# Moving squares ahead of the last piece, a key block across a phase border, and splitting a maximum

## The reference, cut to what matters

```python
def layer(x, cond, l, rope, ctx_kv):
    sh_a, sc_a, g_a, sh_f, sc_f, g_f = adaln_params(cond, mod_w[l], mod_b[l])
    o, k, v = token_mixer(modulate(x, norm_attn[l], sh_a, sc_a), l, rope, ctx_kv)
    x = x + g_a * o
    f = conv_ffn(modulate(x, norm_ffn[l], sh_f, sc_f), w_up[l], conv_w[l], conv_b[l], w_down[l])
    return x + g_f * f, k, v

def modulate(x, norm_w, shift, scale):
    return rms_norm(x, norm_w) * (1.0 + scale) + shift       # rms_norm: mean of squares over the 1024 channels

def conv_ffn(h, w_up, conv_w, conv_b, w_down):
    u = conv(h @ w_up); g, val = jnp.split(u, 2, axis=-1)
    return (jax.nn.silu(g) * val) @ w_down

# grouped-query attention, per head: q, k normed and rotated
p = jax.nn.softmax(jnp.einsum("bhgqd,bhkd->bhgqk", qb, k) * scale, axis=-1)
o = jnp.einsum("bhgqk,bhkd->bhgqd", p, v)
```

## Time and profile before

| | |
|---|---|
| median of three executions | 3475.7 us |
| the profiled execution | 3473.29 us, span 3471.5 us |
| TensorE busy | 3284.7 us (95%) |
| VectorE busy | 1878.1 us (54%) |
| ScalarE busy | 1186.1 us (34%) |
| GpSimd busy | 952.6 us (27%) |
| mean granted TensorE clock | 0.982 of 2.4 GHz |

### The profile page before, as it was taken

The page is one execution under the profiler, slowest core; times in us unless marked ns, Lnnn a source line. Parts: engine busy times, 40 slices in busy tenths (PEclk is TensorE's granted clock), DMA queues, the critical chain, the costliest instruction groups (busy, mean ns, idle before and its releaser), DMA issues. The chain is left out here.

```text
span 3471.5 us, 51842 instructions
## 1 busy us (share of the span) xinstructions
PE 3284.7 (95%) x20797; PEld 3037.5 (87%) x20797; DVE 1878.1 (54%) x2696; ACT 1186.1 (34%) x2113; POOL 952.6 (27%) x730
## 2 busy tenths in 40 slices
PE   6899999997999999999989999998899999999997
PEld 4788888886999999999988877776799999999997
DVE  5555666664275455555555566665336555555456
ACT  3344444444241212222133566655423212122122
POOL 1122222222342222323243122222143222323221
PEclk8999999999999999999999999999899999999999
DMA  6333333423211111111113111101331111111101
GB/s 242 89 108 108 106 113 111 120 80 117 91 62 43 37 42 36 42 42 49 42 43 83 31 32 36 30 24 36 114 95 60 43 36 36 42 54 42 36 31 61
DMA packets 206660, 229.79 MB, mean 66 GB/s; under 512 B 30564, under 2 KB 173533, under 8 KB 205341
## 3 DMA queue, kind: packets, MB, share of 16 engines
q1 hardware_dynamic: 186973, 162.69, 15.6%
q10 hardware_dynamic: 11664, 42.47, 3.8%
q0 software_dynamic: 7856, 22.29, 1.8%
HBM read 181.79 MB, written 31.98 MB: 62 GB/s over the span
## 5 line engine op out<-in xcount | busy, mean ns | idle before, releaser
L192 PE MATMUL psum<-Hh,wh 128*128 128x384 f32 x3264 | 1110.2, 340 | 30.6 <-PEq L498 11.3
L194 PE MATMUL psum<-Hl,wh 128*128 128x384 f32 x3264 | 1097.4, 336 | 0.0
L193 PE MATMUL psum<-Hh,wl 128*128 128x384 f32 x3264 | 1097.1, 336 | 0.0
L311 DVE SCALAR_TENSOR_TENSOR x<-psum,mod,x 128x384 f32<-128x384 f32 (+2 forms) x768 | 376.9, 514 | 633.0 <-PE psum L194 594.0
L192 PEld LDWEIGHTS psum<-Hh,wh 128*128 128x128 f32 x3264 | 617.5, 189 | 41.9 <-issue 32.3
L193 PEld LDWEIGHTS psum<-Hh,wl 128*128 128x128 f32 x3264 | 617.1, 189 | 0.0
L194 PEld LDWEIGHTS psum<-Hl,wh 128*128 128x128 f32 x3264 | 616.7, 189 | 0.0
L907 POOL TENSOR_TENSOR wl<-wr,wh 128x1024 fp32r<-128x1024 f32 x88 | 219.8, 2498 | 970.9 <-ACT wh L803 970.9
L856 ACT ACTIVATE ff_u<-psum 128x768 f32<-128x768 f32 x86 | 70.0, 813 | 1082.0 <-PE psum L194 1082.0
L1074 DVE SCALAR_TENSOR_TENSOR ff_c<-ff_u,par,ff_c 128x1153 f32<-128x1153 f32 x172 | 371.7, 2161 | 15.6 <-DVE ff_c L1071 5.2
L192 PE MATMUL psum<-ff_ah,ff_dh 128*128 128x384 f32 x1056 | 364.3, 345 | 13.2 <-DVE x L311 8.1
(11 more groups left out here) (237 smaller groups left out, 4396.0 us busy)
## 6 DMA issues: line engine op xcount, KB each, us to landing
wr<-w_up SPq DMA_DIRECT2D x88, 512.0 KB, 3.9
ff_dr<-w_down SPq DMA_DIRECT2D x22, 1024.0 KB, 6.0
da_mw<-mod_w ACTq DMA_DIRECT2D x40, 512.0 KB, 3.9
wr<-mod_w ACTq DMA_DIRECT2D x40, 512.0 KB, 4.8
wr<-w_qkv_diff SPq DMA_DIRECT2D x24, 512.0 KB, 19.1
x<-x_save SPq DMA_DIRECT2D x16, 576.0 KB, 6.3
in_mw<-mod_w SPq DMA_DIRECT2D x8, 1024.0 KB, 11.5
Hh<-oh_save SPq DMA_DIRECT2D x14, 576.0 KB, 9.6
```

Source lines behind the costliest of these rows:

```text
L192: pe.matmul(out, w_hi, m_hi, start=start, stop=False)
L193: pe.matmul(out, w_lo, m_hi, start=False, stop=False)
L194: return pe.matmul(out, w_hi, m_lo, start=False, stop=stop)
L311: last = dve.scalar_tensor_tensor(g.x[:, m, lo:hi], g.PS[:, bank, lo - n * NB:hi - n * NB], g.mod[:, gate + m, cond:cond + 1], g.x[:, m, l ...
```

## The change

Three edits.

- **Squares and sums earlier.** ScalarE does the squares of row blocks 0 to 3 of column block 0 ahead of `end_hi(2)`; GpSimd does their sums ahead of the third low part. The two weight copies `next_hi` move from the front of the squares to behind squares 8 and 12.
- **The third key block.** `normed_banks(..., 2, [(0, 0)])` multiplies it at the end of the FFN phase into bank 0, row block by row block as the normed input comes; `project(("K", 0), 2)` is gone from the next phase, and ScalarE's copy of the weights of key pair 1 there no longer waits for it.
- **The maximum of map 0 in two parts.** A new semaphore `s_two` is raised by the matmul that completes banks 0 and 1 of map 0. VectorE takes the maximum of these 768 columns then, that of the last 384 after the whole map, and one instruction takes the lesser of the two negated maxima and multiplies it by the scale. Map 1 and tile 8 stay as they are.

```diff
+    EARLY = 4 if nx else 0
...
                 end_hi(1)
+                for e in range(EARLY):
+                    next_square(e)
                 end_hi(2)
+
+            def next_square(e):
+                act.wait_ge(b.dn_add, DN * LAST + e + 1)
+                nx.square(act, e)
...
             if nx:
-                for j in range(2):
-                    next_hi(j)
-                for e in range(24):
-                    act.wait_ge(b.dn_add, DN * (GROUPS - 1) + e + 1)
-                    nx.square(act, e)
+                for e in range(EARLY, 24):
+                    next_square(e)
+                    if e in (8, 12):
+                        next_hi(e // 4 - 2)
...
                         for n in range(NN):
+                            if n == 2:
+                                for e in range(EARLY):
+                                    nx.add(pool, e)
                             pool.wait_ge(b.end_hi, n + 1)
...
-                for e in range(24):
+                for e in range(EARLY, 24):
                     nx.add(pool, e)
...
-            normed_banks(g, pe, nx, 1, [(0, 4), (1, 7)])[-1].then_inc(b.up_mm, 1)
+            normed_banks(g, pe, nx, 1, [(0, 4), (1, 7)])
+            normed_banks(g, pe, nx, 2, [(0, 0)])[0].then_inc(b.up_mm, 1)
...
-    FIRST = [("K", 0, 2), ("Q", 0, 2), ("K", 1, 0), ("K", 1, 1), ("K", 1, 2),
+    FIRST = [("Q", 0, 2), ("K", 1, 0), ("K", 1, 1), ("K", 1, 2),
...
-    AHEAD = [u for n in range(2) for u in (("K", 0, n), ("Q", 0, n))]
-    AHEAD_BANK = {("K", 0, 0): 3, ("Q", 0, 0): 5, ("K", 0, 1): 4, ("Q", 0, 1): 7}
+    AHEAD = [u for n in range(2) for u in (("K", 0, n), ("Q", 0, n))] + [("K", 0, 2)]
+    AHEAD_BANK = {("K", 0, 0): 3, ("Q", 0, 0): 5, ("K", 0, 1): 4, ("Q", 0, 1): 7, ("K", 0, 2): 0}
...
-                act.wait_ge(b.full, ring.done(last_bank(UNITS[i - 2])))
+                if i > 2:
+                    act.wait_ge(b.full, ring.done(last_bank(UNITS[i - 2])))
...
                             if n == spans[-1][0] and x == 2:
                                 done.then_inc(b.s_mm, 1)
+                            elif (n, m, x) == (1, 0, 2):
+                                done.then_inc(b.s_two, 1)
...
-            project(("K", 0), 2)
...
             def maxima(j, t):
+                if t < QT:
+                    dve.wait_ge(b.s_two, QT * j + t + 1)
+                    dve.reduce_max(b.nm[:, 2, 0:1], g.PS[:, 0:2, 0:NB], AX.XY, negate=True).then_inc(b.mx, 1)
                 for m in range(2):
-                    c = 2 * (TILES * j + t) + m + 1
-                    dve.wait_ge(b.s_mm, c)
-                    dve.reduce_max(b.nm[:, 0, m:m + 1], banks(g, m, t), AX.XY if t < QT else AX.X, negate=True).then_inc(b.mx, 1)
+                    scale = b.r[:, j % 2, t, m:m + 1]
+                    dve.wait_ge(b.s_mm, 2 * (TILES * j + t) + m + 1)
+                    if t < QT and m == 0:
+                        dve.reduce_max(b.nm[:, 0, 0:1], g.PS[:, 2, 0:NB], AX.X, negate=True).then_inc(b.mx, 1)
+                    else:
+                        dve.reduce_max(b.nm[:, 0, m:m + 1], banks(g, m, t), AX.XY if t < QT else AX.X, negate=True).then_inc(b.mx, 1)
...
-                    dve.wait_ge(b.mx, c)
-                    dve.tensor_tensor(b.nm[:, 1, m:m + 1], b.nm[:, 0, m:m + 1], b.r[:, j % 2, t, m:m + 1], ALU.mult).then_inc(b.nmax, 1)
+                    dve.wait_ge(b.mx, maxima_found(j, t, m))
+                    if t < QT and m == 0:
+                        dve.scalar_tensor_tensor(b.nm[:, 1, 0:1], b.nm[:, 0, 0:1], b.nm[:, 2, 0:1], scale, ALU.min, ALU.mult)\
+                            .then_inc(b.nmax, 1)
+                    else:
+                        dve.tensor_tensor(b.nm[:, 1, m:m + 1], b.nm[:, 0, m:m + 1], scale, ALU.mult).then_inc(b.nmax, 1)
```

More of the change, by code:

```diff
@@ L2091, in phase_gqa_attention @@
         "yb": ([P, 2, 2 * P], F32), "y": ([P, 2, 2 * P], F32), "yh": ([P, 2 * P], F32R), "yl": ([P, 2 * P], F32R),
-        "nm": ([P, 2, 2], F32), "l": ([P, 4, 2], F32), "rl": ([P, 2, 2], F32), "wq": ([P, 1], F32),
+        "nm": ([P, 3, 2], F32), "l": ([P, 4, 2], F32), "rl": ([P, 2, 2], F32), "wq": ([P, 1], F32),
         "r": ([P, 2, TT, 2], F32)},
         "tab w_in0 w_in1 w_hi w_lo free0 free1 full free2 free3 free4 ahead side sq_d ck_in ck_d cv_in ko_d v_st k_st ms_d r_d normed kswap swap rope"
-        " s_mm mx nmax exp q_d rl_d pv_out y_d y_split y_out wq_d wo_in0 wo_in1 wo_hi wo_lo o_in")
+        " s_two s_mm mx nmax exp q_d rl_d pv_out y_d y_split y_out wq_d wo_in0 wo_in1 wo_hi wo_lo o_in")
     free = {"F": b.free0, "C": b.free1, 0: b.free2, 1: b.free3, 2: b.free4}
@@ L2581, in normal_keys, with maxima_found @@
                                              ALU.mult).then_inc(b.normed, 1)
+            def maxima_found(j, t, m):
+                return (2 * TILES + QT) * j + 3 * t + (m + 2 if t < QT else m + 1)
             def maxima(j, t):
+                if t < QT:
+                    dve.wait_ge(b.s_two, QT * j + t + 1)
+                    dve.reduce_max(b.nm[:, 2, 0:1], g.PS[:, 0:2, 0:NB], AX.XY, negate=True).then_inc(b.mx, 1)
                 for m in range(2):
-                    c = 2 * (TILES * j + t) + m + 1
-                    dve.wait_ge(b.s_mm, c)
-                    dve.reduce_max(b.nm[:, 0, m:m + 1], banks(g, m, t), AX.XY if t < QT else AX.X, negate=True).then_inc(b.mx, 1)
+                    scale = b.r[:, j % 2, t, m:m + 1]
[4 more added lines that the diff above has]
+                        dve.reduce_max(b.nm[:, 0, m:m + 1], banks(g, m, t), AX.XY if t < QT else AX.X, negate=True).then_inc(b.mx, 1)
                     if t == 0 and m == 0:
                         dve.wait_ge(b.r_d, MEAN["Q", j])
-                    dve.wait_ge(b.mx, c)
-                    dve.tensor_tensor(b.nm[:, 1, m:m + 1], b.nm[:, 0, m:m + 1], b.r[:, j % 2, t, m:m + 1], ALU.mult).then_inc(b.nmax, 1)
+                    dve.wait_ge(b.mx, maxima_found(j, t, m))
[4 more added lines that the diff above has]
+                        dve.tensor_tensor(b.nm[:, 1, m:m + 1], b.nm[:, 0, m:m + 1], scale, ALU.mult).then_inc(b.nmax, 1)
             def sums(j, p):
```

## The result

The changed kernel takes 3459.3 us (median of 5 runs, 3457.8 to 3464.4), the kernel before beside it 3478.9 us: a ratio (of the means) of 0.9949, with a 95% interval from 0.9936 to 0.9963. That is 17.7 us less (13 to 22), where 13.9 us less was forecast. The forecast lies between the two.

A forecast was written before the change was run, and what follows sets the result against it. TensorE, busy 95% of the span, was taken as the bound. Against the profiled 3473.29 us, -2.9 us (squares and key block) and -11.0 us (two-part maximum) gave 3459.4 us, or 3461.8 us as median; range 3455 to 3470 us.

The forecast's parts named there:

- What bounds the kernel: Whole kernel: TensorE is busy 95% of the span, so only its idle and half-clock time can be won.
- Squares and sums: FFN's end: partition sum 4.2 us earlier, spread 7.1 us earlier, VectorE done 6.5 us earlier.
- The lock: FFN's end: GpSimd's early adds delay VectorE's last piece 1.0 us (0 to 3.4); its first low part loses 0.6 us more.
- The weight copies between the squares: FFN's end: ScalarE's moved copies, 1.0 us each, are hidden by GpSimd's queue of adds; uncovered they would cost 2 us.
- The key block in the FFN: FFN's end: 4.2 us of matmuls mostly covered by VectorE; phase ends 0.75 us behind it, border 5.7 us earlier.
- The key block out of attention: Attention's start: removal gains nothing; TensorE idles 8 us for cached keys, then a half-clock query block costs 2.75 us.
- The split: Attention's tile loop: map 0's maximum ends 0.44 us earlier in 25 waiting tiles, 11.0 us in all (9.0 to 13.0).
- The sum: Whole kernel: -2.9 and -11.0 make -13.9 us, 3459.4 us profiled, 3461.8 us as median; chance 0.57.
- The clock term: Attention's start: after the idleness 18 query-block matmuls run at half clock, +2.75 us (0 to 3.7).
- The split gives nothing: Tile loop rival: map 1's wait takes back what map 0's saved, or the first part has no lead; 3472.8 us, chance 0.13.
- Slower: Tile loop rival: VectorE isn't idle, so the extra 0.16 us is paid in all 64 tiles; 3483 us, chance 0.05.
- The FFN's end gives nothing: FFN and attention's start, rival: whole-add locking or attention's slow start eats the gain; 3464.7 us, chance 0.25.

The follow-up runs named there:

- split_alone: Kernel before with only the two-part maximum of map 0 added: 3460.7 us, 0.9974 of the kernel before.
- query_first_banks: Changed kernel with the query block at attention's very start, ahead of both waits, and the work banks dealt out as before: 3457.3 us, 0.9953 of the kernel before.
- key_block_back: Changed kernel with the third key block back at the start of attention: 3454.5 us, 0.9951 of the kernel before.
- split_late: Changed kernel with both parts of map 0's maximum taken only after the whole map: 3477.0 us, 1.0010 of the kernel before.
- squares_alone: Kernel before with only the earlier squares and sums and the moved weight copies: 3468.8 us, 0.9992 of the kernel before.
- after_again: The changed kernel itself, unaltered, measured once more in another series: 3462.0 us, 0.9967 of the kernel before.

## Why the prediction was right, point by point

- **What bounds the kernel.** Right. What the stages gained lies in TensorE's stops, and its half clock, in the two phases named, and the profile of after shows TensorE at 95% of the span as before.
- **Squares and sums.** Right in mechanism. Forecast: sum 4.2 us earlier, spread 7.1 us, VectorE done 6.5 us. Measured: 4.3, 7.2 (26.79 to 19.57) and 6.35 us. No half clock follows (1.00 instead of 0.50). The stop is under 2 us: 0.35. The 4.3 us are the same against both traces of the old code. The other two sizes are in part luck: the prediction took the 17 half-clock matmuls of before for fixed, and split_alone, with the same code there, has 7. Against it the spread is 5.75 us earlier, VectorE's end 5.4 us.
- **The lock.** Forecast 1.0 us for the last piece. GpSimd's last low part ends at +9.6 instead of +8.8 us, 0.8 us later, while three adds of 1.1 us run; 0.28 us of it is the product (0.83 instead of 0.55 us), 0.39 us the instruction at 1792.52 us (1.00 instead of 0.61 us) and 0.10 us the one at 1791.37 us (0.71 us). The upper bound of 3.4 us, a whole add for each, didn't come. The Trainium skill's statement (SBUF — State Buffer, section "SBUF: two separate sides") of an exclusive lock for a whole instruction is in line with the rows that got longer (0.83, 1.00, 1.57 us): an instruction that starts inside an add pays for what is left of it, and not for a whole add. At the second place 0.6 us was forecast. VectorE's first low part takes 1.57 us, 0.6 us more than its counterpart in before, which also met a subtraction of GpSimd, later in its run:

```profile
1815.27 0.98 DVE L438 SCALAR_TENSOR_TENSOR Hl<-ff_c,mod,Hh 128x384 fp32r<-128x384 f32 x1
```

VectorE's lead shrinks from 7.1 us at its first row to 6.35 us at its last. But this too is no fixed price of the edit: in split_alone, with the old code, the same row is 1.57 us.
- **The weight copies between the squares.** Hidden, as said: eight adds follow each other in 9.16 us, 1.145 each.
- **The key block in the FFN.** Forecast: attention starts 5.7 us earlier. Measured: attention's first instruction on VectorE is at +62.18 us, before it was at +67.63 us: 5.45 us (4.5 us against split_alone's +66.70). With the block the phase ends 0.9 us later behind VectorE's last row, for 0.75 us forecast.
- **The key block out of attention.** The wait is there, 8.12 us long and ended by the cached keys' DMA, for a forecast of about 8 us. The query block behind it takes 5.84 us (1857.30 to 1863.14) instead of 6.8: 9 matmuls are at half clock and not 18. That term was oversized by 1 us. In the other kernels with the key block moved and the query block behind the keys it is 6 to 14 matmuls. I had taken the count of the old start of attention over as fixed; it isn't.
- **A step that was missing.** That the key block's place in `FIRST` decides which bank every later block gets. It cost a stop of 1.05 us, and of the loop 1.3 us (query_first_banks, where the places are restored) to 1.7 us (key_block_back, where the block is back as well). The diff showed it: the list lost its first entry, and places go by the index. I read it only as the removal of work. With it, the block's move is a loss of some 4 us by the trace, which the comparison with key_block_back shows; the prediction had the start of it (removing the block gains nothing, and the clock costs 2.75 us) and put the sum with the squares, so that the loss didn't stand out.
- **The split.** Reductions 0.96 and 0.55 us, for 0.96 and 0.56 us forecast. The one thing mis-sized is the combining instruction: 0.22 us instead of the 0.16 us of a multiplication. So a tile gains 0.40 us and not 0.44 us. 20 x 0.40 = 8.0 us for the loop (split_alone: 8.2), and 5 long stops 0.4 us shorter each: 10 us for 11.0. The window in which the lead had to exist (VectorE idle 1.3 us or more) was read rightly: split_late shows 0.53 us for a lead taken as 0.52.
- **The sum.** Terms by the trace: -5.45 at the border, +1.5 to the keys' squares, -6.5 in the loop (-8.2 and +1.7), -4.0 behind it to the loop's end: -14.4 us. Forecast: -5.7 + 2.75 - 11.0 = -13.9 us. That the two are so close is partly luck. The clock term was 1.2 us too dear, and its size changes from trace to trace; the bank's 1.7 us were missing. Of the last -4.0 us the five long stops explain 2.0; the rest is within what that stretch scatters between kernels of equal code there (103 to 107 us with the split in two parts, 107 and 110 us without). And the same code was 17.7 us faster in one series and 11.4 us in another, a gap as large as the largest of these terms.
- **The rivals.** "The split gives nothing" falls: map 1's stop stayed at 0.26 us, and split_alone has 0.9974. "Slower" falls, and split_late shows what it would have looked like. "The FFN's end gives nothing" isn't quite dead: squares_alone is 5.6 to 6.7 us ahead by the trace at the keys' squares, and its time is 0.9992 (0.9983 to 1.0002). The gain is there in the stages; how much of it reaches the time, between 0 and 6 us, stays open.

## What to carry to other kernels

A step that only fills a wait is worth nothing when it is moved away, and it can cost: ask what its engine does in its place, at which clock it comes back, and what else depends on its position in a list. A reduction over several banks can start as soon as the first of them are complete, if its engine idles until then; its gain in a tile is the lead less the cost of one more instruction, and the next engine in the chain sets the end of it. Trace differences of 1 to 3 us between two executions need a look at the granted clock first, and the stage that repeats many times is the one to measure in.

## What the runs showed of the hardware that was not expected

- The stretches of half clock are not tied to the code. The same code (after, after_again) had one of ten matmuls at +1.3 us or none, and 9 or 13 half-clock matmuls behind the same wait of 8.1 and 8.4 us. Each matmul of 384 columns in it costs 0.145 us.
- The query block ran at a granted clock of 1.00 right behind the FFN, and at about 0.5 where 3 us of idleness lay ahead of it (3.05 us, 17 matmuls); when it ran first, the 3.70 us of idleness behind it sent the next matmuls to half clock instead.
- Four DMAs of cached keys with nothing ahead of them on their queue still landed only some 5.7 us after TensorE had run idle: two of them 1.6 and 1.7 us after their issue, two 3.9 and 4.0 us after it, together with a load of 512 KB that GpSimd had issued just ahead of these two. No run was made without that load there.
- A stop of TensorE shown as 0.18 us costs 0.27 us from start to start.
- What VectorE and GpSimd cost each other at the end of the FFN is regular. In the 14 traces from 1780 to 1830 us, all 86 instructions of VectorE that read two tensors in SBUF and started inside an add or subtraction of GpSimd ended 0.40 to 0.45 us behind the end of that one, whatever their start; by themselves those of 384 and 385 columns take 0.55 to 0.62 us. VectorE's 384-column adds to `g.x`, which read one tensor in PSUM and one in SBUF, stayed at 0.60 to 0.62 us beside GpSimd's work. It goes the other way too: GpSimd's 384-column add takes 0.99 to 1.03 us by itself, and, but for 3 of 96, 1.13 to 1.34 us when it starts inside such an instruction of VectorE.
